# Attention heads in pairs, first scores inside the last projection, norm2 rows and router weights loaded during the heads

## The reference

```
# attention of layer 1 (latent queries alone, keys of latent and context)
q, k, v = split(h @ w_qkv)            # 16 query heads, 4 key heads, of 64
q = rms_norm(q, q_gain); k = rms_norm(k, k_gain)      # then rotary positions for latents
s = einsum("bqkgd,bskd->bkgqs", qg, k) * ATT_SCALE
p = softmax(s, axis=-1)
o = einsum("bkgqs,bskd->bqkgd", p, v)
x = x + g1 * (o @ w_o)
# then
f = rms_norm(x, norm2_g) * (1 + sc2) + sh2
group, expert logits = f @ w_group + b_group, f @ w_router + b_router
# top group, top 2 of its 8 experts; each expert: (silu(f @ w_gate) * (f @ w_up)) @ w_down
x = x + g2 * moe(f)
```

## Time and profile before

| what | value |
|---|---|
| median of 3 runs | 1873.03 us (1872.93 to 1875.63) |
| profiled execution | 1872.92 us, its span 1871.1 us |
| mean granted TensorE clock | 0.956 of full speed |
| PE, DVE, ACT busy, share of the span | 83%, 29%, 22% |
| mean DMA rate over the span | 310 GB/s |
| attention and output projection, layer 1 | about 1161 to 1361 us from the span's start |
| experts of layer 1, first turn | 1376.94 us |

### The profile page before, as it was taken

The page is one execution under the profiler, slowest core; times in us unless marked ns, Lnnn a source line. Parts: engine busy times, 40 slices in busy tenths (PEclk is TensorE's granted clock), DMA queues, the critical chain, the costliest instruction groups (busy, mean ns, idle before and its releaser), DMA issues.

```text
span 1871.1 us, 21703 instructions
## 1 busy us (share of the span) xinstructions
PE 1562.1 (83%) x8634; PEld 825.4 (44%) x8634; DVE 535.0 (29%) x1134; ACT 415.9 (22%) x827; POOL 254.1 (14%) x267
## 2 busy tenths in 40 slices
PE   3999999999999889788877773977789888777774
PEld 2434446666545555444434341433455544434341
DVE  2433347777533320000000003455331000000001
ACT  2221147888501101000000002145110100000000
POOL 2000013443210101010101002100110110101001
PEclk9899999999999999999999997978889999999997
DMA  9477759995342799999999996710469999999994
GB/s 362 159 287 285 271 198 256 309 318 207 125 161 78 279 396 421 421 421 422 421 421 421 422 419 237 271 49 1 167 267 382 419 419 421 420 422 420 420 421 178
DMA packets 166141, 579.74 MB, mean 310 GB/s; under 512 B 22290, under 2 KB 77986, under 8 KB 143296
## 3 DMA queue, kind: packets, MB, share of 16 engines
q1 hardware_dynamic: 145072, 531.25, 71.8%
q0 software_dynamic: 15248, 27.62, 4.3%
q10 hardware_dynamic: 5760, 20.06, 3.3%
HBM read 550.60 MB, written 49.77 MB: 321 GB/s over the span
## 4 chain that ended last, share of the span: by engine, by line
PE 48%; DMA 38%; DVE 6%; issue 3%; ACT 3%; POOL 1%; SPq 0%; ACTq 0%; POOLq 0%; DVEq 0%
DMA mem<-in_moe_w_down_dram 33%; PE bank L588 9%; PE bank L1777 8%; PE bank L1764 7%; PE bank L937 6%; PE bank L882 3%; PE bank L2027 3%; PE bank L331 2%; PE bank L905 2%; DMA mem<-in_mod_w_dram 2%; DMA mem<-in_moe_w_gate_dram 1%; ACT mem L987 1%; PE bank L2053 1%; PE bank L900 1%; PE bank L2133 1%
## 5 line engine op out<-in xcount | busy, mean ns | idle before, releaser
L1764 PE MATMUL bank<-mem 128*64 128x256 f32 x4160 | 475.2, 383 | 86.0 <-DMA mem<-in_moe_w_up_dram 38.5
L1764 PEld LDWEIGHTS bank<-mem 128*64 128x64 f32 x4160 | 304.4, 137 | 257.0 <-DMA mem<-in_moe_w_up_dram 59.8
L1777 PE MATMUL bank<-mem 128*64 128x512 f32 x1040 | 254.3, 634 | 89.9 <-DMA mem<-in_moe_w_down_dram 80.7
L1920 DVE COPY mem<-bank 128x256 f32<-128x256 f32 x65 | 27.6, 425 | 690.4 <-PE bank L1771 690.4
L1715 POOL DMA_INDIRECT ys_dram<-mem x65 | 64.7, 996 | 864.8 <-ACT mem L1870 491.1
L1777 PEld LDWEIGHTS bank<-mem 128*64 128x64 f32 x1040 | 76.0, 144 | 226.0 <-issue 132.9
L1870 ACT ACTIVATE mem<-bank 128x512 f32<-128x512 f32 x65 | 38.8, 597 | 611.4 <-PE bank L1777 611.4
L588 PE MATMUL bank<-mem 128*128 128x512 f32 x384 | 173.1, 604 | 1.4 <-DMA mem<-in_ssd_w_in_dram 1.4
L588 PEld LDWEIGHTS bank<-mem 128*128 128x128 f32 x384 | 71.8, 192 | 100.0 <-issue 96.8
L882 PE MATMUL bank<-mem 128*128 128x512 f32 x256 | 115.2, 593 | 0.0
L937 PE MATMUL bank<-mem 128*128 128x512 f32 x256 | 112.3, 595 | 1.8 <-issue 0.9
(11 more groups left out here) (277 smaller groups left out, 1430.3 us busy)
## 6 DMA issues: line engine op xcount, KB each, us to landing
mem<-in_moe_w_up_dram SPq DMA_DIRECT2D x65, 2048.0 KB, 27.3
mem<-in_moe_w_down_dram SPq DMA_DIRECT2D x65, 2048.0 KB, 26.8
mem<-in_moe_w_gate_dram SPq DMA_DIRECT2D x65, 2048.0 KB, 26.4
mem<-in_mod_w_dram SPq DMA_DIRECT2D x24, 2048.0 KB, 8.9
ys_dram<-consts SPq DMA_DIRECT2D x54, 512.0 KB, 7.8
mem<-in_ssd_w_in_dram SPq DMA_DIRECT2D x10, 2048.0 KB, 9.4
mem<-ac_dram ACTq DMA_DIRECT2D x32, 512.0 KB, 5.5
mem<-in_ssd_w_out_dram SPq DMA_DIRECT2D x4, 2048.0 KB, 11.8
```

The source lines that it names most:

```text
L1764: mm = nc.tensor.matmul(bank[half * BR:(half + 1) * BR, 0:HF], lhsT=x[:, k], rhs=w[:, k, half * HF:(half + 1) * HF], start=(k == 0), stop= ...
L1777: mm = nc.tensor.matmul(bank[half * BR:(half + 1) * BR, :], lhsT=ht[:, k % 2, k // 2 * BR:(k // 2 + 1) * BR], rhs=w[:, k, half * COLS:(hal ...
```

## The change

**Pairs.** An item is now a pair j of two heads of one tile (j = 2p + t). Scores of both heads, both maxima, one bias operation (L2293) for both, both Exps, one reciprocal for both. The scores of pair j+2 stand on PE ahead of the turns of pair j, and ScalarE does the Exps of pair j+1 ahead of the copies of pair j.

**Start.** The last projection is split in two halves of four k steps; the scores of pairs 0 and 1 stand between them. The turns of the third and fourth key tile stand together. The third query tile is turned after the scores of pair 2. ScalarE does one Exp on a column at the start of the attention, so that its table is there.

**End.** The first part of the output projection does six of eight steps, then `values(7)`, then the two others.

**norm2.** The preparation is a function of its own (`norm2_prep_dve`), in layer 1 called ahead of the last output copy. POOL starts its loads once the fourth query tile is done (`at_q` at 4); two bias loads and one row load wait for the last scores. Buffers are moved to where they are free by then.

```diff
-                pool.wait_ge(at_o, QH // 2)
+                pool.wait_ge(at_q, 4)
             mod_wait(pool, NG if l else MODG)
+            pool.dma_start(wrt[l][:, :, 0:EG], a["moe_w_group"][l].rearrange("(k p) n -> p k n", p=P)).then_inc(n2_in, 16)
+            pool.dma_start(wrt[l][:, :, EG:], a["moe_w_router"][l].rearrange("(k p) n -> p k n", p=P)).then_inc(n2_in, 16)
             pool.dma_start(gain2, a["norm2_g"][l:l + 1, :].to_broadcast([P, D])).then_inc(n2_in, 16)
-            pool.dma_start(wrt[:, :, 0:EG], a["moe_w_group"][l].rearrange("(k p) n -> p k n", p=P)).then_inc(n2_in, 16)
-            pool.dma_start(wrt[:, :, EG:], a["moe_w_router"][l].rearrange("(k p) n -> p k n", p=P)).then_inc(n2_in, 16)
+            for s in range(ns):
+                pool.dma_start(mA[l][:, s, :], mod_dram[l, s:s + 1, 4 * D:5 * D].to_broadcast([P, D])).then_inc(n2_in, 16)
+            if l:
+                pool.wait_ge(n2_in, N2_IN[1][0])
+                pool.wait_ge(at_s, 2 * QH)
             pool.dma_start(brt[:, 0:EG], a["moe_b_group"][l:l + 1, :].to_broadcast([P, EG])).then_inc(n2_in, 16)
             pool.dma_start(brt[:, EG:], a["moe_b_router"][l:l + 1, :].to_broadcast([P, E])).then_inc(n2_in, 16)
             for s in range(ns):
-                pool.dma_start(mA[:, s, :], mod_dram[l, s:s + 1, 4 * D:5 * D].to_broadcast([P, D])).then_inc(n2_in, 16)
-                pool.dma_start(mB[:, s, :], mod_dram[l, s:s + 1, 3 * D:4 * D].to_broadcast([P, D])).then_inc(n2_in, 16)
+                pool.dma_start(mB[l][:, s, :], mod_dram[l, s:s + 1, 3 * D:4 * D].to_broadcast([P, D])).then_inc(n2_in, 16)
...
+        def norm2_prep_dve(dve, l):
+            dve.wait_ge(n2_in, N2_IN[l][0])
...
-            def scores(i):
-                p, t, hh = item(i)
-                lo = HD * hh
-                if i >= 4:
-                    pe.wait_ge(at_p, i - 3)
-                nc.tensor.matmul(psum[SB[i % 4]][:, :], lhsT=qT[lo:lo + HD, p, t * P:(t + 1) * P],
+            def scores(j):
+                p, t = divmod(j, 2)
+                if j >= 2:
+                    pe.wait_ge(at_p, 2 * j - 2)
+                for hh in range(2):
+                    nc.tensor.matmul(psum[SB[j % 2][hh]][:, :], lhsT=qT[HD * hh:HD * (hh + 1), p, t * P:(t + 1) * P],
+                                     rhs=kT[HD * hh:HD * (hh + 1), p // 2, :], start=True, stop=True).then_inc(at_s, 1)
...
             unit_wait(pe, U_QKV + 2)
-            project(1, 0, 6)
+            pe.wait_ge(at_ke, 3)
+            project(1, 0, 4)
             turn_k(2)
-            project(1, 1, 7)
             turn_k(3)
             pe.wait_ge(at_ke, 4)
-            turn_q(2, 4)
+            project(1, 1, 5, range(4))
             pe.wait_ge(at_te, 6)
-            pe.wait_ge(at_qe, 4)
-            for i in range(4):
-                scores(i)
...
+            scores(0)
+            scores(1)
+            project(1, 1, 5, range(4, KD))
+            for j in range(NJ):
+                if j + 2 < NJ:
+                    if j + 2 == NJ // 2:
+                        pe.wait_ge(at_te, 8)
+                    scores(j + 2)
+                if j in (0, 3):
+                    turn_q(2 + j // 3)
+                turn(j)
+                if j >= 2 and j % 2 == 0:
+                    if j <= 4:
+                        pe.wait_ge(at_te, 6 + j // 2)
+                    values(j // 2 - 1)
...
             unit_wait(pe, U_WO)
-            out_part(0, 0, range(KD))
+            pe.wait_ge(at_p, NI2)
+            pe.wait_ge(at_o, NPAIRS - 2)
+            out_part(0, 0, range(NPAIRS - 2))
+            values(NPAIRS - 1)
+            pe.wait_ge(at_o, NPAIRS - 1)
+            out_part(0, 0, [NPAIRS - 2])
+            pe.wait_ge(at_o, NPAIRS)
+            out_part(0, 0, [NPAIRS - 1])
...
+            nc.scalar.activation(craw[:, 0, 0:1], mhalf[:, 0:1], ACT.Exp)
...
+            exps(0)
+            exps(1)
             evac_q(3)
...
+            for j in range(NJ):
+                if j >= 1 and j + 1 < NJ:
+                    exps(j + 1)
+                turned(j)
+                if j in (0, 3):
+                    turned_q(2 + j // 3)
...
+            for j in range(NJ):
+                share(j)
+                if j == 1:
+                    query_mean(3)
+                    query_turn(3)
+                if j + 2 < NJ:
+                    top(j + 2)
+                if j >= 3 and j % 2:
+                    output((j - 3) // 2)
+            norm2_prep_dve(dve, 1)
             output(NPAIRS - 1)
```

More of the change, by code:

```diff
@@ L2035, in turn_q @@
                     c = (4 * u + r) * P
-                    tp = nc.tensor.transpose(psum[bank][:, r * P:(r + 1) * P], qrow[:, t, c:c + P], ident)
+                    tp = nc.tensor.transpose(psum[Q_AT[j]][:, r * P:(r + 1) * P], qrow[:, t, c:c + P], ident)
                 tp.then_inc(at_tp, 1)
@@ L2196, in attn_act @@
             evac_kv(1)
-            turned_q(0, 1, 0)
-            turned_q(1, 2, 1)
+            turned_q(0)
+            turned_q(1)
             evac_kv(2)
@@ L2204, in attn_act @@
             turned_k(2)
+            turned_k(3)
+            exps(0)
+            exps(1)
             evac_q(3)
[L2206 to L2220 removed]
+            for j in range(NJ):
[4 more added lines that the diff above has]
+                    turned_q(2 + j // 3)
         def attn_dve(dve):
@@ L2270, in key, with top, share @@
                 dve.wait_ge(at_k, t + 1)
-            def top(i):
-                dve.wait_ge(at_s, i + 1)
-                link(dve, V.tensor_reduce(amax[:, i:i + 1], psum[SB[i % 4]][:, :], AX, ALU.max))
-                V.tensor_scalar(abias[:, i:i + 1], amax[:, i:i + 1], qk_rs[:, item_col(i)], -1.0, ALU.mult,
-                                ALU.mult).then_inc(at_m, 1)
-            def share(i):
-                dve.wait_ge(at_p, i + 1)
-                link(dve, V.reciprocal(ainv[:, i:i + 1], asum[:, i:i + 1]))
-                V.tensor_scalar(prob[:, i % 4, :], prob[:, i % 4, :], ainv[:, i:i + 1], None, ALU.mult).then_inc(at_n, 1)
+            def top(j):
+                c = pair_cols(j)
+                for hh in range(2):
+                    i = 2 * j + hh
+                    dve.wait_ge(at_s, i + 1)
+                    ins = V.tensor_reduce(amax[:, i:i + 1], psum[SB[j % 2][hh]][:, :], AX, ALU.max)
+                link(dve, ins)
+                if j >= NJ // 2:
+                    dve.wait_ge(at_rs, 7 + j % 2)
+                V.scalar_tensor_tensor(abias[:, 2 * j:2 * j + 2], amax[:, 2 * j:2 * j + 2], -1.0, qk_rs[:, c:c + 2],
+                                       ALU.mult, ALU.mult).then_inc(at_m, 1)
+            def share(j):
+                dve.wait_ge(at_p, 2 * j + 2)
+                link(dve, V.reciprocal(ainv[:, 2 * j:2 * j + 2], asum[:, 2 * j:2 * j + 2]))
+                for hh in range(2):
+                    b, i = 2 * (j % 2) + hh, 2 * j + hh
+                    V.tensor_scalar(prob[:, b, :], prob[:, b, :], ainv[:, i:i + 1], None, ALU.mult).then_inc(at_n, 1)
             def output(p):
@@ L2302, in attn_dve @@
             stream_rows_dve(dve, 1)
-            query(0)
+            query_mean(0)
+            query_turn(0)
             stream_evac_dve(dve, 1)
-            query(1)
+            query_mean(1)
+            query_turn(1)
             for t in range(NT):
                 key(t)
-            query(2)
-            dve.wait_ge(at_rs, 7)
+            query_mean(2)
+            query_turn(2)
             top(0)
             top(1)
-            for i in range(NI2):
-                if i == 5:
-                    query(3)
-                    dve.wait_ge(at_rs, 8)
-                if i + 2 < NI2:
-                    top(i + 2)
-                share(i)
-                if i >= 4 and i % 4 == 3:
-                    output(i // 4 - 1)
+            for j in range(NJ):
[8 more added lines that the diff above has]
+            norm2_prep_dve(dve, 1)
             output(NPAIRS - 1)
```

183 lines of the change are left out of this document (79 added, 104 removed).

## The result

| | before | after |
|---|---|---|
| median of 4 runs on the same chip | 1873.9 us | 1826.62 us (1825.31 to 1829.99) |
| ratio, 95% interval | 1 | 0.9749 (0.9733 to 0.9766) |
| span of the profiled execution | 1871.1 us | 1823.3 us |
| mean granted TensorE clock | 0.956 | 0.967 |

The account below looks back on a forecast made before the run. Expert weight transfers end a third of the span, but compute engines bound the heads and set when experts start. Reaching the shift rows 43.2 us earlier plus 1.6 for the cold step takes 44.7 off 1872.92: 1828.2 us, range 1822 to 1843.

Parts of the forecast that it names:

- shift rows: PE's work behind the output projection, waiting for norm2's loads and preparation; to be reached at 1298.32, not 1341.48: 43.2 us.
- The gap behind query tile 3: Early heads: PE idles 3.0 us ahead of turns 2 while VectorE spends 3.75 us on query tile 3.
- clock charge: TensorE's clock falls once at the early stall; 2.1 us for turns and scores of one pair at double, bounds 0 and 6.
- The period: Two pairs of steady heads: 6.06 us of PE work plus 0.48 of stall, 6.54; bounds 6.06 and 10.96.
- Rows of norm2: Loads leave near 1235, land by 1255; preparation hides beside the output projection, else costs up to 2.9 us; removes the 8.2 wait.
- The cold step: The projection step behind the shift rows no longer starts at the low clock: 5.00 - 3.44 = 1.6 us saved.
- One to one to the end: Time saved in heads and output projection moves the expert stage and the end equally: a constant 44 us shift.
- Layer 0 and the table load: Layer 0's preparation only changes its own order, and the Exp table load moved ahead had cover enough: both gain nothing.
- The oscillating clock: Rival: small pauses keep TensorE's clock at 0.83 in the heads, a cycle takes 7.8 us; 1836 us, chance 0.15.
- Handshakes as the period: Rival: something unseen keeps two pairs of heads at 10.96 us; 1861 us, chance 0.06.
- Slower at the low level throughout: Rival: PE stays at 1.2 GHz through heads and projection; 1887 us, chance 0.03.
- the hidden transfer: Rival: expert weight transfers fix the end by themselves, so the gain is lost; 1873 us, chance 0.02.

Follow-up runs that it names:

- copy-first experiment: Changed kernel with VectorE's output copy ahead of the maxima of the next pair; 1828.98 us.
- norm2 only: Kernel before with only the new norm2 loads and preparation, heads as before; 1864.64 us, ratio to before 0.996.
- the repeat: The unaltered changed kernel measured again, beside a version with two further edits on one chip; 1829.37 us, ratio to before 0.9762.
- single heads: Changed kernel with VectorE and ScalarE handing over one head at a time again, scores still ahead; 1835.01 us, ratio to before 0.9785.
- scores-behind run: Changed kernel with the scores of pair j+2 behind the turns of pair j instead of ahead; 1853.30 us, ratio to before 0.9893.
- projection whole: Changed kernel with the first scores behind the whole last projection instead of between its halves; 1828.62 us.

## Why the prediction was right

Step by step, from the start of the projection, predicted and measured in the first trace after:

| step | predicted | measured |
|---|---|---|
| scores 0 | 11.18 | 11.27 |
| turns 2, behind the gap | 26.4 (gap 3.0) | 26.29 (gap 3.01) |
| pair 4 begins | 34.0 | 33.22 |
| two pairs in the steady state | 6.54, stall 0.48 | 6.53, stall 0.41 |
| turns 14 | 68.2 | 66.98 |
| shift rows | 87.8 | 86.62 |

- **The gap behind query tile 3** was sized to 0.01. Its clock charge was 2.1 with bounds of 0 and 6; it was 1.51 in one execution and 2.78 in another of the same kernel, most of it on turns and values rather than on turns and scores. That 2.1 lies between them is a good middle and no more: nothing in the prediction could tell which of them an execution pays. The late estimate of pair 4 follows from that; the first period also had no stall (turns 4 start as scores 6 end), another 0.4.
- **The period.** The path over VectorE was summed as 2.57 against 2.09 of PE's own work. The copy-first experiment shows that this path set it: 0.34 taken from it makes the period 0.33 shorter. That the scores ahead free the period is shown by their removal (10.41).
- **Rows of norm2.** The wait of 8.18 is gone. Summed by itself it is right (norm2 only: 8.94 to the shift rows and 1.4 behind them). The sum by positions on PE held although the two parts are not independent: adding up the parts each from the old order would have missed 5 to 7 us.
- **The cold step**, predicted 1.6: shift rows to experts' turn took 35.30 before and 33.10 after, 2.2. The step itself is 1.5 of that. Of the rest, 0.3 is that the shift rows themselves run faster now (0.31 against 0.64 in the earlier trace rows) and 0.4 the eight records of constants (5.70 against 6.08), which vary anyway.
- **One to one to the end**: 494.3 us from the experts' turn to the end of the span in both traces. Units went out from 1287.7 on and were not late.
- **Layer 0 and the table load**: nothing, as predicted; the second is shown by the run, the first by rows that agree to 0.02 from 135 to 632 us, beyond layer 0's preparation at 536.
- **Sum.** Measured 46.6 in the stretch, predicted 44.7. A further 1.2 of the 47.8 between the spans arose before the stretch, where executions differ anyway. Between medians on one chip the gain was 47.3 in the first comparison and 44.6 in the repeat, so the closeness of 44.7 to either is within what executions differ by.

**The rivals.** The oscillating clock did not come: 1.00 in every 4 us window from 1242 to 1306. The Trainium skill, TensorE: Matmul & The Clock Gate, section "A second HAM failure mode: psum-queue depth-cycling", reports it of a bf16 kernel whose small pauses between groups, with cycled banks, were frequent enough; the prediction took that as a rule. The traces do not bear it out as a rule by itself: banks cycle here in every pair, and stalls of 0.41 in 6.53 us, or 0.71 in 6.99 (single heads), left the clock at 1.00; with the same banks and stalls of 2.50 in 10.41 it was 0.77. Handshakes as the period (1861): with 6.53 for two pairs this did not come, and the scores-behind run shows what it would have looked like. Slower at the low level throughout, and the hidden transfer, are excluded by the windows and by the 494.3.

## What to carry to other kernels

Ask of each engine-to-engine loop which result the busiest engine waits for and how many independent pieces it issues between; moving the next piece's first step ahead of the wait was worth some 26 us here, merging the small instructions and handing over pairs some 5. Add up a change by positions on the engine that ends last, not by parts: a wait removed is worth more when the work that hid it moves away. And where the start of a stage differs by several us between executions, compare the stage inside the traces.

## What the runs showed of the hardware

- **A gap's length alone did not decide whether the clock fell.** 2.44 us behind a long unbroken stretch left it at 1.00 (projection whole); 3.01 us brought 0.68 (after); in the single-heads kernel 1.84 us in the tail, behind periods with 0.71 of stall at a granted 1.00, was followed by values of 3.39, while 1.48 in the kernel after was followed by 1.95. What decides between them stays open.
- **The price of one gap varies between executions** of the same program: 1.51 and 2.78 us, and 1.4 to 2.9 over five traces that are alike on PE up to this gap of 3.01 us.
- **After 13.35 us of idleness** the first eight records of the projection took 6.41 instead of 3.68.
- **A table load cost nothing in either of two places with idle time around it**: 1.28 us moved by 85 us (1135.04 in the trace after, 1219.96 without the early Exp) left turns 2 at 26.29 from the projection's start. One run shows this.
